# Gathering block one's tokens expert by expert, and placing two experts' weights elsewhere

## The reference, cut to what matters

```python
def _hier_moe(h, w_rg, b_rg, w_re, b_re, w_gate, w_up, w_down):
    t = h.reshape(B * S, D)                       # 256 x 1024, after an RMS norm with gain ffn_norm_g
    ...                                           # best group of 4, best 2 of its 8 experts
    for g in range(N_GROUPS):
        a = jnp.einsum('td,edf->tef', t, w_gate[g])
        b = jnp.einsum('td,edf->tef', t, w_up[g])
        m = jax.nn.silu(a) * b * combine[:, g, :, None]
        y = y + jnp.einsum('tef,efd->td', m, w_down[g])
```

## Time and profile before

| what | value |
|---|---|
| median of 3 runs | 921.93 us |
| the profiled execution | 920.49 us |
| its span (first to last instruction) | 918.6 us |
| TensorE | 860.4 us busy (94%) |
| VectorE | 503.8 us busy (55%) |
| ScalarE | 349.9 us busy (38%) |
| moved by DMA | 288.46 MB, 314 GB/s over the span |
| block one's experts, from gate and up of expert 0 to the last scatter | 310.5 to 521.1 us |

### The profile page before, as it was taken

The page is one execution under the profiler, slowest core; times in us unless marked ns, Lnnn a source line. Parts: engine busy times, 40 slices in busy tenths (PEclk is TensorE's granted clock), DMA queues, the critical chain, the costliest instruction groups (busy, mean ns, idle before and its releaser), DMA issues.

```text
span 918.6 us, 14920 instructions
## 1 busy us (share of the span) xinstructions
PE 860.4 (94%) x5634; PEld 552.9 (60%) x5634; DVE 503.8 (55%) x1112; ACT 349.9 (38%) x689; POOL 22.2 (2%) x41
## 2 busy tenths in 40 slices
PE   8999999999999998998877899999899999999994
PEld 6778558888976534443333389877565455455552
DVE  5877568465466566333333576888854533333335
ACT  5674435446355322222222457744521111111113
POOL 1010111000000000000000000000000000000000
PEclk9999999999999999999999999999999999999998
DMA  9655895547618899999999996530969899999991
GB/s 354 250 203 225 326 373 202 193 159 273 265 49 309 322 415 382 426 423 426 424 428 422 424 362 240 201 138 1 371 212 413 341 418 427 422 425 425 427 413 50
DMA packets 30242, 288.46 MB, mean 314 GB/s; under 512 B 3144, under 2 KB 5608, under 8 KB 8944
## 3 DMA queue, kind: packets, MB, share of 16 engines
q1 hardware_dynamic: 26688, 281.40, 75.9%
q0 software_dynamic: 1136, 3.74, 1.2%
q10 hardware_dynamic: 2368, 2.64, 0.9%
HBM read 286.70 MB, written 1.06 MB: 313 GB/s over the span
## 4 chain that ended last, share of the span: by engine, by line
PE 68%; DMA 13%; DVE 11%; ACT 4%; issue 2%; SPq 0%; DVEq 0%; ACTq 0%
PE bank L1154 13%; DMA ring<-in_experts 11%; PE bank L1174 8%; PE bank L735 8%; PE bank L737 7%; PE bank L736 7%; PE bank L1202 6%; PE bank L1159 3%; PE bank L1166 2%; DVE ring_r L525 2%; PE bank L1110 2%; PE bank L861 1%; DMA ring<-in_ada 1%; PE bank L1256 1%; DMA ring<-in_lat 1%
## 5 line engine op out<-in xcount | busy, mean ns | idle before, releaser
L525 DVE TENSOR_TENSOR ring_r<-ring,ring_r 128x1024 fp32r<-128x1024 f32 (+1 forms) x84 | 99.4, 1212 | 65.9 <-ACT ring_r L518 65.8
L1154 PE MATMUL bank<-ring,arena 128*64 128x256 f32 x1024 | 117.6, 382 | 0.6 <-DVE arena L2494 0.6
L518 ACT ACTIVATE ring_r<-ring 128x1024 fp32r<-128x1024 f32 (+1 forms) x84 | 85.0, 1046 | 68.3 <-PE bank L737 67.4
L735 PE MATMUL bank<-HT_r,ring_r 128*128 128x256 f32 x352 | 102.0, 290 | 1.3 <-DVE arena_r L2062 0.7
L737 PE MATMUL bank<-HT_r,ring_r 128*128 128x256 f32 x352 | 99.6, 283 | 0.0
L1174 PE MATMUL bank<-ring,arena 128*64 128x512 f32 (+1 forms) x496 | 93.7, 604 | 0.7 <-DVE arena L2569 0.6
L1154 PEld LDWEIGHTS bank<-ring,arena 128*64 128x64 f32 x1024 | 71.1, 137 | 38.1 <-issue 6.1
L1769 ACT ACTIVATE arena<-bank 128x256 f32<-128x256 f32 (+1 forms) x65 | 31.8, 489 | 139.8 <-PE bank L1154 82.1
L736 PE MATMUL bank<-XN_r,ring_r 128*128 128x256 f32 x288 | 81.4, 283 | 0.0
L2542 DVE SCALAR_TENSOR_TENSOR arena<-bank,arena 128x512 f32<-128x512 f32 x33 | 24.8, 750 | 101.4 <-PE bank L1174 101.4
L1202 PE MATMUL bank<-arena_r 64*128 64x512 f32 x504 | 75.4, 417 | 4.3 <-DVE arena_r L2549 3.8
(11 more groups left out here) (490 smaller groups left out, 1416.7 us busy)
## 6 DMA issues: line engine op xcount, KB each, us to landing
ring<-in_experts SPq DMA_DIRECT2D x62, 2048.0 KB, 15.4
ring<-in_experts SPq DMA_DIRECT2D x62, 1024.0 KB, 12.2
ring<-in_ada SPq DMA_DIRECT2D x12, 2048.0 KB, 11.1
ring<-in_win SPq DMA_DIRECT2D x5, 2048.0 KB, 15.2
ring<-in_hy SPq DMA_DIRECT2D x3, 2048.0 KB, 17.9
ring<-in_mk SPq DMA_DIRECT2D x2, 2048.0 KB, 9.0
ring<-in_mv SPq DMA_DIRECT2D x2, 2048.0 KB, 10.1
ring<-in_wo SPq DMA_DIRECT2D x2, 2048.0 KB, 7.9
```

Source lines behind the costliest of these rows:

```text
L518: nc.scalar.activation(R(h), w, ACT.Copy).then_inc(sem("w_high"), 1)
L525: nc.vector.tensor_tensor(R(w), w, R(h), ALU.subtract).then_inc(sem("w_low"), 1)
L735: mm(ps, R(ah), R(bh), start=first, stop=False)
L1154: last = mm(gu_bank[g * wide:(g + 1) * wide, 0:256], xw[:, k, :], w[k // 4][:, k % 4, g * 256:(g + 1) * 256], start=k == 0, stop=k == KD - 1)
```

## The change

Block one no longer makes `xsT`. The tokens of one expert's window are gathered in that expert's turn: TensorE multiplies `XN`, as it is, by the 32 columns of the selection matrix that belong to the window (`picked`), 8 chunks of channels x 2 halves of the tokens = 16 plain float32 matmuls with 128 stationary columns and 32 moving columns (`tokens_of`). VectorE writes them with the gain to `xwin` (`scaled_tokens`) and copies the next 32 columns of the matrix from `sorted_at` to `picked` (`pick`). In step e the gather of expert e+1 stands where the filler matmuls stood. The first window's columns are built directly, ahead of the whole matrix, and TensorE gathers expert 0 before step 0 and expert 1 behind the bias rows. The rounded parts of `XN`, the `gx1` stages and their evacuations go in block one; block two keeps its way.

The arena's first 8192 columns, which held `xsT` and the rounded parts, are now free early. Expert 4's gate and up halves go to columns 4096 to 8191, issued between experts 1 and 2 once the last product of cross attention is done (`xv3`). Expert 5's go to columns 0 to 4095 right behind expert 3, with no wait of their own, and its down half to `HT` after `rt1`. Small tiles move (`ranked`, `turned`, and the tables of the overflow count, to `X`), and `cnt1` and `cns1` swap banks.

```diff
@@ SyncE: experts
-                for e in range(RING):
+                for e in range(RING):
+                    if b == 0 and e == 2:
+                        filled(f"xv{XH - 1}")
+                        for q in range(2):
+                            beside_ring(0, q)
+                    in_ring(e)
...
-                    sp.wait_ge(sem("xn_low"), TT)
+                    for q in range(2):
+                        beside_ring(1, q)
                     filled("rt1")
-                    for q in range(2):
-                        beside_ring(0, q)
-                    filled("cns1")
                     sp.dma_start(outside[1][1], w[RING + 1, :, GU:SLOT]).then_inc(sem("outside1"), 16)
-                    for q in range(2):
-                        filled("gx1", 4 * q + 3)
-                        beside_ring(1, q)
@@ TensorE: moe
+                def tokens_of(i):
+                    for k in range(KD):
+                        for t in range(TT):
+                            last = mm(list_bank[:, k * wide:(k + 1) * wide], XN[:, t, k * P:(k + 1) * P], picked[:, i, t, :],
+                                      start=t == 0, stop=t == TT - 1)
+                    return last
+
+                def gather_window(e, i):
+                    pe.wait_ge(sem("picked"), e + 1)
+                    pe.wait_ge(sem("xwin1"), e)
+                    tokens_of(i).then_inc(sem("gathered"), 1)
@@ TensorE: step
-                        if b == 1:
-                            for _ in range(1 if isinstance(e, int) and e < unrolled else 3):
-                                mm(list_bank[:, 0:256], ident, T("iota")[:, 0:256], start=True, stop=True)
+                        if b == 1 and not (isinstance(e, int) and e == last_step):
+                            gather_window(e + 1, (r + 1) % 2)
...
                     if first_window:
                         beside_first()
+                        if b == 1:
+                            gather_window(1, 1)
@@ TensorE: ahead of step 0
+                if b == 1:
+                    ready(pe, "cnt1")
+                    pe.wait_ge(sem("picked"), 1)
+                    tokens_of(0).then_inc(sem("gathered"), 1)
@@ VectorE: moe
+                def tokens_in(e, i):
+                    dve.wait_ge(sem("gathered"), e + 1)
+                    if not (isinstance(e, int) and e < 2):
+                        dve.wait_ge(sem("gu_done1"), e - 1)
+                    scaled_tokens(i).then_inc(sem("xwin1"), 1)
+
+                def pick(e, i):
+                    s = window(e, i)
+                    V.tensor_copy(picked[:, i], sorted_at[:, :, bass.ds(s, WIN[1])]).then_inc(sem("picked"), 1)
...
+                    places(picked[:, 0, 0, :], WIN[1], 0)
+                    link(places(picked[:, 0, 1, :], WIN[1], 1))
+                    second_places(picked[:, 0, 0, :], WIN[1], 0)
+                    second_places(picked[:, 0, 1, :], WIN[1], 1).then_inc(sem("picked"), 1)
+                    places(sorted_at[:, 0, 0:NPAIR], NPAIR, 0)
+                    link(places(sorted_at[:, 1, 0:NPAIR], NPAIR, 1))
+                    second_places(sorted_at[:, 0, 0:NPAIR], NPAIR, 0)
+                    second_places(sorted_at[:, 1, 0:NPAIR], NPAIR, 1)
+                    tokens_in(0, 0)
...
+                    if b == 1:
+                        tokens_in(e, i)
+                        if not (isinstance(e, int) and e == NE - 1):
+                            pick(e + 1, 1 - i)
+                        return
```

More of the change, by code:

```diff
@@ L1104, in moe @@
                 full(last, f"cns{b}")
[L1105 removed]
+                if b == 2:
+                    occupy("gx2", 0, 2)
                 def gather(k, t):
@@ L1113, in gather, with gather_all @@
                         full(last, f"gx{b}", k)
[L1115 to L1122, removed]
-                    for t in range(TT):
[L1124 to L1127, removed]
+                def gather_all():
+                    for t in range(TT):
+                        pe.wait_ge(sem("sel2"), t + 1)
+                        pe.wait_ge(sem("xn_low"), t + 1)
+                        for k in range(3):
+                            gather(k, t)
+                    for k in range(3, KD):
+                        gx.append(take(pe, "gx2", k))
+                        for t in range(TT):
+                            gather(k, t)
+                    for k in range(KD - 1):
+                        ready(pe, "gx2", k)
+                    pe.wait_ge(sem("pad"), 5)
+                if b == 2:
+                    gx = [take(pe, "gx2", k) for k in range(3)]
+                    gather_all()
                 def beside_first():
@@ L1296, in moe @@
                         pe.wait_ge(sem(f"extra_x{b}"), j + b)
+                        if b == 1:
+                            pe.wait_ge(sem("y_low1"), NE)
+                            tokens_of(0).then_inc(sem("gathered"), 1)
+                            pe.wait_ge(sem("xwin1"), j + NE + 1)
                         pe.wait_ge(sem(f"extra_w{b}"), j * 16 + 16)
@@ L1742, in moe @@
                 A_(gex, cand4, ACT.Exp).then_inc(sem("logit_exp"), 1)
[L1743 to L1749, removed]
+                for k in range(0, KD * (b - 1), 2):
+                    ps = got(act, "gx2", k)
+                    free(A_(xsT[:, k, 0:NPAIR], ps[:, :], ACT.Identity, scale=gain(k), bias=shift(k)), "gx2", k)
                 gu_bank, guT_bank, d_bank, list_bank = expert_banks(b)
@@ L2466, in moe, with places, second_places @@
                 iota = T("iota")
[L2467 to L2470, removed]
+                def places(to, n, t):
+                    return V.tensor_scalar(to, iota[:, 0:n], pos1[:, t:t + 1], None, ALU.is_equal)
+                def second_places(to, n, t):
+                    return V.scalar_tensor_tensor(out=to, in0=iota[:, 0:n], scalar=pos2[:, t:t + 1], in1=to, op0=ALU.is_equal, op1=ALU.add)
+                if b == 2:
+                    for t in range(TT):
+                        link(places(R(sel[:, t, :]), NPAIR, t))
+                        second_places(R(sel[:, t, :]), NPAIR, t).then_inc(sem("sel2"), 1)
+                else:
+                    places(picked[:, 0, 0, :], WIN[1], 0)
[7 more added lines that the diff above has]
+                    tokens_in(0, 0)
+                    V.memset(sorted_at[:, :, NPAIR:NPAIR + WIN[1]], 0.0).then_inc(sem("pad"), 1)
                 dve.wait_ge(sem("logit_exp"), 2 * b - 1)
@@ L2482, in moe @@
                 V.tensor_copy(starts[0:1, :], ps[0:1, 3 * NE:4 * NE])
+                if b == 1:
+                    dve.wait_ge(sem("pad"), 2)
+                    pick(1, 1)
                 free(of_tokens(ps), f"cns{b}")
@@ L2511, in moe @@
                 wide, gu_sum, sg, hb, xwin = expert_tiles(b)
[L2512 to L2520, removed]
+                if b == 2:
+                    V.memset(xsT[:, :, NPAIR:SORTED], 0.0).then_inc(sem("pad"), 1)
+                    dve.wait_ge(sem("pad"), 3)
+                    second = window(1, 1)
+                    for k in range(3, KD, 2):
+                        sorted_out(k)
+                    dve.wait_ge(sem("pad"), 5)
+                    for k in range(0, KD):
+                        ready(dve, "gx2", k)
+                    V.tensor_copy(xwin[:, 1], xsT[:, :, bass.ds(second, wide)]).then_inc(sem("xwin2"), 1)
                 free(slots_out(listed, got(dve, f"slots{b}")), f"slots{b}")
                 ready(dve, f"slots{b}")
-                if b == 2:
+                if b == 1:
+                    tokens_in(1, 1)
+                    pick(2, 0)
+                else:
                     for j in range(2):
@@ L2702, in moe @@
                         if b == 1:
+                            dve.wait_ge(sem("gathered"), j + NE + 1)
+                            scaled_tokens(0).then_inc(sem("xwin1"), 1)
                             dve.wait_ge(sem("extra_gT1"), j + 1)
```

60 lines of the change are left out of this document (33 added, 27 removed).

## The result

The changed kernel takes 1008.9 us (median of 4 runs, 1005.5 to 1010.9), the kernel before 922.1 us beside it: a ratio of 1.0937, 95% interval 1.0902 to 1.0972. I had forecast slower, 968 us with a range of 959 to 978. The direction was right and the size was not: 87 us came, 46 were forecast.

The account below looks back on a forecast made before the run. Weights bound the loop before; TensorE would after. Expert 31's start 46.9 us later, less 0.8, gives 46.1; on 920.49 that is 966.6, plus 1.4 from execution to median: 968 us, range 959 to 978.

Parts of the forecast that it names:

- 32 x 0.112 us: Gather in each step: 32 loads of the stationary operand at 0.112 us each, 3.58 us, whatever the moving columns.
- a step of 8.11: Expert step on TensorE: 4.46 us remaining plus 3.65 us for the gather, with the weights' 7.40 us falling behind.
- Part 1: The gather in each step: filler out, 32 loads in, making a TensorE-paced step of 8.11 us.
- the 4.46 us for the rest of the step: TensorE's step without waits, 5.85 us, less the filler's 1.39 us.
- Part 3: The loop: steps 2 to 30 take 29 x 8.11 = 235.2 us, so expert 31's gate and up start 46.9 us later.
- The rival on the handoff: VectorE's pick of the next columns comes too late; TensorE waits 1 us per step: 997 us, chance 0.05.
- The start: Before the loop: expert 0 starts 4.35 us earlier, but step 2 at 323.7 instead of 318.46, 5.2 us later.
- Early transfers: Weights of experts 4 and 5 issued earlier on SyncE's queue fill the hole of slice 12 but buy nothing.
- Break-even: Gather time at which expert 31's gate and up start at 512.45 as before: 2.14 us, or 0.067 us per record.
- 2.94 us per step: Expert steps: 1.55 us of TensorE idle plus 1.39 us of filler, usable before TensorE becomes the bound.
- rival 1: In the gather, moving columns set the price, weights stay the bound and it gets faster: 912 us, chance 0.03.
- The 0.8 us of `ada11`: Longer steps give back the wait for `ada11`, at most 1.0 us, taken as 0.8 off the total.

Follow-up runs that it names:

- the run with 128 columns: The changed kernel with each gather matmul moving the same 32 columns four times over, the later copies overwritten or unread: 970.6 us.
- the pair by rows: The version gathered by rows with the transfers of experts 4 and 5 at their old places, against that version with early transfers: 937.7 us beside 937.0.
- by rows: The changed kernel's gather with roles swapped: picked columns stationary, 512 token columns moving in four column groups, then turned by four matmuls: 936.95 us.
- the gather by rows with expert 1 first: The version gathered by rows with expert 1's gather and turning ahead of the slot lists and bias rows instead of behind: 931.3 us, 1.0108 times before.
- the half gather: The changed kernel gathering only chunks 0 to 3 of 8, with 128 moving columns (16 loads), the other channels stale: 927.7 us.

## Why the prediction was right or wrong

**What bounds, and what the gather costs: right.** 32 x 0.112 us and a step of 8.11 were the argument; steps with the clock up measure 8.07, and 8.13 with 128 columns. TensorE took the bound over, gate and up no longer waited for weights, and the range held the time of the run in which the clock stayed up (970.6).

**The clock: the step that failed.** Part 1 read "TensorE's granted clock is 1.00" in a stretch of the kernel before and priced gate and up, scatter and down at that level, with a run of 32 matmuls of 32 columns put where fillers of 256 columns had stood. The filler was taken out at its time alone (1.39 us). What it also did in the kernel before, holding the clock up, was neither priced nor among the rivals, and nor was a fall of the clock behind the gather. So the 4.46 us for the rest of the step, and with it Part 3's 29 x 8.11 = 235.2 us, were too small: steps 2 to 30 took 264.9 us. The clock measures 9.13 - 8.13 = 1.0 us per step, 29 us over 29 steps, and 5.7 us more at the start. The rival on the handoff had the wrong mechanism at nearly the right size (997 us); TensorE did not idle in the loop.

The Trainium skill (TensorE: Matmul & The Clock Gate, What's actually happening) says that the clock has two states and that a monitor of TensorE's recent activity chooses. The traces agree on the two levels: 1.00 in the run with 128 columns from 330 us on, and 0.50 from 310 to 330 us in the run with the filler behind the gather. The same page's case of a clock that swings (HAM oscillation) is a loop that waits on DMA. Here the windows row shows TensorE busy for 50.00 of 50.00 us while the clock falls, which that case does not cover.

**The start: late by 10 us.** 323.7 forecast, 333.58 measured. 2.3 us of it lie ahead of the stage. The run with 128 columns has 325.79, with one short fall of the clock, so my handoffs were off by 2 us at most; the rest, 5.5 us or more, is the clock.

**Early transfers worth nothing: right,** within 2 us in the pair by rows and more loosely in the other. My reason was half of it: by rows, where the weights set the end of the loop again, they did not pay either, which is what the in-order queue would give.

**Break-even: wrong.** I put 2.94 us per step as "free", and in rival 1 a gather of 2.14 us as break-even, with the stream of weights unbroken from 318 us. A gather of 1.9 us measured 927.7, where this gave 909 to 918, and the stream was not unbroken: 335 GB/s from 335 to 370 us. The early steps count nearly in full, through the slots, and only the late ones have room.

**The 0.8 us of `ada11`** did not come off the time. The waits for its weights are gone, but in the profiled executions the end of block one and the whole time both moved by 86.6 us.

**The range: its sum was off.** Minus 4 or plus 7 us over the steps and 2 us for the start give 962 to 977, where 959 to 978 were stated. It changes nothing here.

No version here is clearly faster than the kernel before. The best with the changed layout is the gather by rows with expert 1 first, 1.0108 times before. Using the two places outside the ring a second time, which the free arena would allow and which would lengthen the queue's lead, was not tried.

## What to carry to other kernels

When an edit replaces wide matmuls or fillers by a long run of narrow ones, price the clock of what comes behind the run, not the run's own time alone; where the load of the stationary operand sets the pace, moving more columns, even useless copies, is nearly free and here gave back 38 us between the medians. Before you call time under the DMA's pace free, follow the queue: with few slots and an in-order queue an early step's delay reaches the end, and the loop's mean step, not the transfer's time, is the bar.

## What the runs showed of the hardware

- The granted clock fell to the lower level while TensorE's records left no gap: 0.86 over 50 us with 50.00 us busy. It stayed at 1.00 in the loop with the same 32 loads and 128 columns each, and with the 32 loads in two halves.
- It also fell behind waits: in the half gather TensorE waited 2.75 us for the weights of expert 31, and gate and up then took 3.26 us instead of 1.92, at a granted clock of 0.56.
- A plain float32 matmul of 128 x 128 stationary took 0.112 us per load with 32 moving columns and 3.67 / 32 = 0.115 with 128.
- One filler of 0.5 us behind each gather made the kernel 30 us slower (1039.4 beside 1008.9): about 14 us are its own time, and the fall of the clock came in 28 of 29 steps instead of 19.
